# The residual moved out to DRAM during the expert stage, and a fourth expert's first weights loaded into its place

## The reference, cut to what matters

```
x2 = x + concat(RMSNorm_A(attention), RMSNorm_B(conv)) @ W_out
h  = RMSNorm(x2)
group = argmax(h @ w_group)                       # 1 of 4
two experts of the 8 in the group, by h @ w_expert, with gates
for each chosen expert e:
    hid = silu(h @ w_gate[e]) * (h @ w_up[e])     # 1024 -> 512
    y  += gate * (hid @ w_down[e])                # 512 -> 1024
out = RMSNorm_final(x2 + y)
```

## Time and profile before

| | us |
|---|---|
| median of 3 runs | 884.88 (883.33 to 888.36) |
| profiled execution | 884.24 |
| its span in the trace | 882.4 |
| TensorE busy | 834.6 (95%) |
| VectorE / ScalarE / GpSimd busy | 379.2 / 239.7 / 136.9 |
| queue of SyncE's transfers | 240.39 MB, 69.8% of 16 engines' span |
| HBM read / written | 247.01 MB / 24.20 MB |

### The profile page before, as it was taken

One profiled execution on the slowest core, in us unless ns is written; L12 is line 12 of the kernel. 1 busy time (PEld: TensorE's weight loads), 2 busy tenths in 40 slices (PEclk: granted clock), 3 DMA queues, 4 the chain that ended last, 5 costly groups with the idle time before them and its releaser, 6 DMA issues.

```text
span 882.4 us, 15903 instructions
## 1 busy us (share of the span) xinstructions
PE 834.6 (95%) x5910; PEld 560.5 (64%) x5911; DVE 379.2 (43%) x712; ACT 239.7 (27%) x490; POOL 136.9 (16%) x287
## 2 busy tenths in 40 slices
PE   6999999999999999899999889999999999999974
PEld 5988877778777888665555455555555555555531
DVE  5599999985563545721111111111111111111246
ACT  4423211557876133111111111111111111111122
POOL 3300110000000010121222122112221122211112
PEclk9999999999999999999999999999999999999988
DMA  7454644122171489499999999999999999999875
GB/s 194 103 134 118 192 160 167 48 85 61 48 239 49 189 349 384 169 407 418 418 420 419 420 420 421 419 421 419 421 419 420 418 421 419 420 410 419 368 288 183
DMA packets 81010, 262.42 MB, mean 297 GB/s; under 512 B 19017, under 2 KB 44873, under 8 KB 56394
## 3 DMA queue, kind: packets, MB, share of 16 engines
q1 hardware_dynamic: 62976, 240.39, 69.8%
q0 software_dynamic: 7888, 18.78, 5.5%
q10 hardware_dynamic: 10106, 2.71, 1.3%
HBM read 247.01 MB, written 24.20 MB: 307 GB/s over the span
## 4 chain that ended last, share of the span: by engine, by line
PE 53%; DMA 18%; DVE 16%; SPq 8%; issue 2%; ACT 1%; POOL 1%; POOLq 0%; DVEq 0%; ACTq 0%
DMA big<-in_w_up 16%; PE ps L1381 12%; PE ps L1418 8%; DVE big L1843 8%; SPq L804 8%; PE ps L1260 8%; PE ps L1124 7%; PE ps L1384 3%; PE ps L1396 2%; PE ps L1176 2%; PE ps L1143 2%; PE ps L1372 1%; PE ps L1155 1%; DVE w_split L1780 1%; PE ps L1469 1%
## 5 line engine op out<-in xcount | busy, mean ns | idle before, releaser
L2131 DVE TENSOR_TENSOR big<-ps,big 64x256 f32<-64x256 f32 x78 | 33.2, 426 | 380.5 <-ACT big L1700 380.4
L1384 PE MATMUL ps<-ring,big 128*64 128x256 f32 x704 | 156.1, 380 | 3.6 <-DMA ring<-in_w_up 3.4
L1381 PE MATMUL ps<-ring,big 128*64 128x256 f32 x704 | 156.2, 379 | 1.3 <-issue 1.2
L1124 PE MATMUL ps<-hT,w_split 128*128 128x256 f32 (+1 forms) x744 | 136.5, 340 | 0.5 <-DVE big L1812 0.5
L1381 PEld LDWEIGHTS ps<-ring,big 128*64 128x64 f32 x704 | 96.0, 137 | 56.6 <-issue 12.1
L1124 PEld LDWEIGHTS ps<-hT,w_split 128*128 128x128 f32 x744 | 113.0, 189 | 21.0 <-issue 7.6
L1384 PE MATMUL ps<-big 128*64 128x256 f32 x544 | 121.5, 380 | 5.1 <-DMA big<-in_w_up 5.1
L1381 PE MATMUL ps<-big 128*64 128x256 f32 x544 | 121.5, 380 | 0.0
L1384 PEld LDWEIGHTS ps<-ring,big 128*64 128x64 f32 x704 | 96.2, 137 | 8.0 <-DMA ring<-in_w_up 4.9
L1381 PEld LDWEIGHTS ps<-big 128*64 128x64 f32 x544 | 74.1, 137 | 39.2 <-issue 9.0
L1700 ACT ACTIVATE big<-ps 64x256 f32<-64x256 f32 x78 | 29.3, 375 | 245.3 <-PE ps L1384 245.3
(11 more groups left out here) (269 smaller groups left out, 1166.8 us busy)
## 6 DMA issues: line engine op xcount, KB each, us to landing
ring<-in_w_gate SPq DMA_DIRECT2D x44, 1024.0 KB, 27.5
ring<-in_w_up SPq DMA_DIRECT2D x44, 1024.0 KB, 28.3
ring<-in_w_down SPq DMA_DIRECT2D x44, 1024.0 KB, 28.7
big<-in_w_gate SPq DMA_DIRECT2D x20, 1024.0 KB, 27.7
big<-in_w_up SPq DMA_DIRECT2D x20, 1024.0 KB, 28.2
big<-in_w_down SPq DMA_DIRECT2D x20, 1024.0 KB, 28.1
w_raw<-in_w_in SPq DMA_DIRECT2D x20, 512.0 KB, 4.0
results<-spare POOLq DMA_DIRECT2D x12, 512.0 KB, 3.8
```

Source lines behind the costliest of these rows:

```text
L1124: mm = pe.matmul(ps[:, n % 2, 0:size], w_split[:, sub, hi_w, k, :], hT[:, k // 4, hi_h, k % 4, cols], **flags)
L1381: pe.matmul(ps[0:BLK, 6 * h, 0:FH], xT[:, k % (KD // 2), q, :], gate_w[s][:, k, fs], start=(k == 0), stop=(k == KD - 1))
L1384: mm = pe.matmul(ps[BLK:2 * BLK, 6 * h + 1, 0:FH], xT[:, k % (KD // 2), q, :], up_w[s][:, k, fs], start=(k == 0), stop=(k == KD - 1))
L2131: nc.vector.tensor_tensor(hb[:, fs], ps[BLK:2 * BLK, 6 * h + 1, 0:FH], sG[:, fs], ALU.mult).then_inc(hb_ready[h], 1)
```

## The change

- `AT_ONCE` is 4: experts 0 to 3 have places 0 to 3. The ranks of the other one-block places are shifted by one.
- Each tile of `x` is stored to a DRAM tensor `x2_rows` when it is complete (`keep_x2`).
- When two tiles have been stored and are no longer read, one piece of expert 3's weights is loaded into their place (`load_lent`; `lent` is a view of `x` as three pieces). The pieces are gate half 0, up half 0 and gate half 1.
- Place 3 is multiplied with these three pieces (`in_lent`) and with its other three in slot 0. The slot's own first three pieces so come free for place 6: they are loaded while place 0 ends, and place 6's other three behind place 3. From place 9 on `load_expert` is as before.
- Behind the last weights and ahead of the final gain, the six tiles of `x` are loaded back. The last stage waits for `tile_in[t]` to reach 96.

```diff
--- before.py
+++ after.py
@@ -74,10 +74,12 @@
 MAXPAIRS = (MAXB - 7) // 2
 
 
-PLACES = [((0, 3, 1), E - 3, 1), ((8, 27, 3), 6, -1), ((9, 25, 3), 12, -1), ((7, 26, 3), 19, -1), ((3, 7, 1), 20, 1), ((27, 32, 1), 24, 1)]
-AT_ONCE = 3
+PLACES = [((0, 4, 1), E - 4, 1), ((8, 27, 3), 6, -1), ((9, 25, 3), 12, -1), ((7, 26, 3), 19, -1), ((4, 7, 1), 20, 1), ((27, 32, 1), 23, 1)]
+AT_ONCE = 4
 NB = MAXB + 2
 SLOTS = 3
+
+LENT = 3
 CONSTS = 16 + len(PLACES)
 
 RPBW = 127
@@ -424,6 +426,8 @@
 
     h_rows = nc.dram_tensor("h_rows", (2 * T, D // 2), F32, kind="Internal").ap()
     results = nc.dram_tensor("results", (4 * T, D // 2), F32, kind="Internal").ap()
+
+    x2_rows = nc.dram_tensor("x2_rows", (T, D), F32, kind="Internal").ap()
     h_whole, results_whole = (a.rearrange("(r s) d -> r (s d)", s=2) for a in (h_rows, results))
 
     def rows_of(x_p, x_s, t):
@@ -511,6 +515,9 @@
         gate_w = [g[:, 0:KD * F].rearrange("p (k f) -> p k f", k=KD) for g in gus]
         up_w = [g[:, KD * F:].rearrange("p (k f) -> p k f", k=KD) for g in gus]
         down_w = [d.rearrange("p (k d) -> p k d", k=KF) for d in dns]
+
+
+        lent = x.rearrange("p t d -> p (t d)").rearrange("p (b k f) -> p b k f", b=LENT, k=KD // 2)
 
         taken_at = [(slot2_gu if t < 4 else slot2_dn)[:, 2 * (t % 4) * D:2 * (t % 4 + 1) * D].rearrange("p (j d) -> p j d", j=2)
                     for t in range(NT)]
@@ -672,6 +679,7 @@
         gate_in = [[sem(f"gate_in{s}{q}") for q in range(2)] for s in range(SLOTS)]
         up_in = [[sem(f"up_in{s}{q}") for q in range(2)] for s in range(SLOTS)]
         dn_in = [[sem(f"dn_in{s}{q}") for q in range(2)] for s in range(SLOTS)]
+        lent_in = [sem(f"lent_in{b}") for b in range(LENT)]
         xt_ps, xt_ready, y_done, y_evac = sem("xt_ps"), sem("xt_ready"), sem("y_done"), sem("y_evac")
 
         xb_in, y_out = ([sem(f"{what}{q}") for q in range(2)] for what in ("xb_in", "y_out"))
@@ -796,21 +804,28 @@
                 for q in range(2):
                     yield dn_in[s][q], down_w[s], w_down, slice(q * KF // 2, (q + 1) * KF // 2)
 
+            def weights_of(e, w, ks):
+                if w is w_down:
+                    return w[0, bass.ds(e, 1), ks.start * P:ks.stop * P, :].rearrange("e (p k) d -> p (e k) d", p=P)
+                return w[0, bass.ds(e, 1)].rearrange("e (p k) f -> p (e k) f", p=P)[:, ks, :]
+
             def load(e, landed, to, w, ks):
-                if w is w_down:
-                    src = w[0, bass.ds(e, 1), ks.start * P:ks.stop * P, :].rearrange("e (p k) d -> p (e k) d", p=P)
-                else:
-                    src = w[0, bass.ds(e, 1)].rearrange("e (p k) f -> p (e k) f", p=P)[:, ks, :]
-                sp.dma_start(to[:, ks, :], src).then_inc(landed, 16)
+                sp.dma_start(to[:, ks, :], weights_of(e, w, ks)).then_inc(landed, 16)
 
             def load_some(e, s, first, end):
                 for l in list(in_order(s))[first:end]:
                     load(e, *l)
 
+            def expert_at(place):
+                return sp.value_load(table[0:1, bass.ds(place + (3 * E + 2), 1)], min_val=0, max_val=E - 1)
+
+            def end_of(place):
+                return sp.value_load(table[0:1, bass.ds(place + 2 * E, 1)], min_val=1, max_val=MAXB)
+
             def load_expert(i, s):
                 place = SLOTS * i + s
-                e = sp.value_load(table[0:1, bass.ds(place + (3 * E + 2), 1)], min_val=0, max_val=E - 1)
-                end = sp.value_load(table[0:1, bass.ds(place + (2 * E - SLOTS), 1)], min_val=1, max_val=MAXB)
+                e = expert_at(place)
+                end = end_of(place - SLOTS)
                 sp.wait_ge(gu_half, end)
                 load_some(e, s, 0, 2)
                 sp.wait_ge(gu_done[1], end)
@@ -858,12 +873,53 @@
                 load(1, *l)
             load(0, *pieces[0][5])
 
+
+            def keep_x2(t):
+                sp.wait_ge(x2_done, OUT.index((OUT_CHUNKS - 1, t)) + 1)
+                sp.dma_start(x2_rows[t * P:(t + 1) * P, :], x[:, t, :]).then_inc(tile_in[t], 16)
+
+            def load_lent(b):
+                for t in (2 * b, 2 * b + 1):
+                    sp.wait_ge(tile_in[t], 48)
+                sp.wait_ge(sq2, 2 * b + 2)
+                sp.wait_ge(h2_ready, 2 * b + 2)
+                sp.wait_ge(x2t_done, 2 * b + 2)
+                _, _, w, ks = pieces[0][b]
+                sp.dma_start(lent[:, b], weights_of(SLOTS, w, ks)).then_inc(lent_in[b], 16)
+
+            for t in range(NT):
+                keep_x2(t)
+            for b in range(LENT):
+                load_lent(b)
+
             sp.wait_ge(table_ready, 2)
-            with sp.Fori(1, E // SLOTS) as i:
+
+            ahead, end = expert_at(2 * SLOTS), end_of(0)
+            sp.wait_ge(gu_half, end)
+            load_some(ahead, 0, 0, 2)
+            sp.wait_ge(gu_done[1], end)
+            load_some(SLOTS, 0, 3, 4)
+            load_some(ahead, 0, 2, 3)
+            sp.wait_ge(y_done, end)
+            load_some(SLOTS, 0, 4, 6)
+            for s in range(1, SLOTS):
+                load_expert(1, s)
+            ahead, end = expert_at(2 * SLOTS), end_of(SLOTS)
+            sp.wait_ge(gu_done[1], end)
+            load_some(ahead, 0, 3, 4)
+            sp.wait_ge(y_done, end)
+            load_some(ahead, 0, 5, 6)
+            load_some(ahead, 0, 4, 5)
+            for s in range(1, SLOTS):
+                load_expert(2, s)
+            with sp.Fori(3, E // SLOTS) as i:
                 for s in range(SLOTS):
                     load_expert(i, s)
             for place in range(E // SLOTS * SLOTS, E):
                 load_expert(place // SLOTS, place % SLOTS)
+
+            for t in range(NT):
+                sp.dma_start(x[:, t, :], x2_rows[t * P:(t + 1) * P, :]).then_inc(tile_in[t], 16)
 
             sp.wait_ge(gates_ps, 1)
             sp.dma_start(fin_g, bass.AP(final_g.tensor, 0, [[0, P], [1, D]])).then_inc(norms_in, 16)
@@ -1372,17 +1428,17 @@
                     mm = pe.transpose(ps[:, 4, k * P:(k + 1) * P], xb[:, k * P:(k + 1) * P], ident[:])
                 mm.then_inc(xt_ps, 1)
 
-            def gate_up(s, target, q, h):
+            def gate_up(gate, up, q, h):
 
                 fs = slice(h * FH, (h + 1) * FH)
-                for k in range(q * KD // 2, (q + 1) * KD // 2):
-                    if h == 0 and k % (KD // 2) == 0:
-                        pe.wait_ge(gate_in[s][q], target)
-                    pe.matmul(ps[0:BLK, 6 * h, 0:FH], xT[:, k % (KD // 2), q, :], gate_w[s][:, k, fs], start=(k == 0), stop=(k == KD - 1))
-                    if h == 0 and k % (KD // 2) == 0:
-                        pe.wait_ge(up_in[s][q], target)
-                    mm = pe.matmul(ps[BLK:2 * BLK, 6 * h + 1, 0:FH], xT[:, k % (KD // 2), q, :], up_w[s][:, k, fs],
-                                   start=(k == 0), stop=(k == KD - 1))
+                for k in range(KD // 2):
+                    flags = dict(start=(q == 0 and k == 0), stop=(q == 1 and k == KD // 2 - 1))
+                    if h == 0 and k == 0:
+                        pe.wait_ge(gate[0], gate[1])
+                    pe.matmul(ps[0:BLK, 6 * h, 0:FH], xT[:, k, q, :], gate[2][:, k, fs], **flags)
+                    if h == 0 and k == 0:
+                        pe.wait_ge(up[0], up[1])
+                    mm = pe.matmul(ps[BLK:2 * BLK, 6 * h + 1, 0:FH], xT[:, k, q, :], up[2][:, k, fs], **flags)
                 if q:
                     mm.then_inc(gu_done[h], 1)
                 elif h:
@@ -1397,12 +1453,22 @@
                                       hb[:, h * FH + k:(h + 1) * FH:2], ident[0:BLK, 0:BLK])
                 mm.then_inc(ht_ps[h], 1)
 
-            def expert_block(b, s, target):
+            def in_slot(s, target, head):
+
+                k0, k1 = slice(0, KD // 2), slice(KD // 2, KD)
+                return [((gate_in[s][0], head, gate_w[s][:, k0, :]), (up_in[s][0], head, up_w[s][:, k0, :])),
+                        ((gate_in[s][1], head, gate_w[s][:, k1, :]), (up_in[s][1], target, up_w[s][:, k1, :]))]
+
+            def in_lent(target):
+                return [((lent_in[0], 16, lent[:, 0]), (lent_in[1], 16, lent[:, 1])),
+                        ((lent_in[2], 16, lent[:, 2]), (up_in[0][1], target, up_w[0][:, KD // 2:KD, :]))]
+
+            def expert_block(b, s, target, halves):
 
                 pe.wait_ge(xt_ready, b + 1)
                 for q in range(2):
                     for h in range(2):
-                        gate_up(s, target, q, h)
+                        gate_up(*halves[q], q, h)
                 turn_hidden(b, 0)
 
                 pe.wait_ge(xb_copied, b + 2)
@@ -1425,12 +1491,12 @@
                 first = pe.value_load(table[0:1, bass.ds(place + E, 1)], min_val=0, max_val=MAXB - 1)
                 return n, first
 
-            def blocks(n, first, s, target):
+            def blocks(n, first, s, target, halves):
                 with pe.Fori(0, n) as j:
-                    expert_block(first + j, s, target)
-
```

(28 more changed lines are left out.)

## The result

The changed kernel takes 888.91 us (median of 10 runs, 886.58 to 890.21), the kernel before 884.66 beside it (10 runs, 883.33 to 888.36). The ratio is 1.0044 with a 95% interval of 1.0033 to 1.0056: slower by 0.44%, clear of noise with these runs and still inside the 0.5% that the prediction counted as the same. The forecast was 888.2, with a range of 882.0 to 893.0. The profiled execution took 889.17 us with a span of 887.3, which is 4.9 us more span than before.

What follows compares the result with a forecast made beforehand. The DMA engines' weight stream was taken to set the pace of the expert stage. From 884.24, -7.5 (stream), +5.9 (late start) and +5.6 (read-back) sum to +4.0: 888.2 us, range 882.0 to 893.0.

Steps and rivals of the forecast that it cites:

- 7.5 less in the stream: Expert weights after 369: three pieces, 3.15 MB, leave the stream, saving 7.5 us at 417 GB/s.
- 5.9 for a late start: Before the first blocks: slowed transfers on the router's chain delay block 0's end, block 1 and the next weight triggers by 5.9 us.
- 5.6 for the read-back: Behind the last weights: reloading 3.15 MB adds 7.5 us on the slowest DMA engine, 1.9 idle absorbs some; cost 5.6 us.
- The DMA engines set the pace: Expert stage: TensorE's 13.7 us of losses are waits for weights; an earlier or lighter stream saves time out of those.
- ScalarE's stores of h: Tiles 4 and 5, before the first gather: slowed beside x's stores, 0 to +3 us, taken as +0.9.
- The gather of block 0: Router's chain, issued at 360.1: slowed beside stores, 0 to +5.3 us, taken as +2.0, with 0.7 given back by VectorE.
- That of block 1: Second gather on the router's chain: beside the lent loads it takes 6.9 us in place of 3.2, +3.7.
- A: End of the kernel: the read-back fits before the results and the lead is kept, 882.6 to 878.6; chance 0.14.
- B: Start: gathers suffer under +1 us each, only the spill of 1.9 to 3 us is paid, 884.8, no change; chance 0.17.
- C: Start is worse: stores of h held up 3 us, gathers take 8.2, 12 us in place of 5.9, 894; chance 0.12.
- D: Expert stage: TensorE is the limit, start delay adds in full +5.9, read-back 0 to 5.6, 890 to 896; 0.09 with E.
- E: Start: x's region not free until 345, lent pieces issued behind block 0, bytes only change places, about 886 to 890; 0.09 with D.

Runs made afterwards that it cites:

- the copy later: Changed kernel with VectorE's copy of block 1's rows, and its part in block 0's first hidden half, moved behind the router's one-hot work: 886.29 us, ratio 1.0014.
- the stores alone: Kernel before plus only the six stores of x to DRAM, with no lent loads and no read-back: 889.4 us, ratio 1.0046.

## Why the prediction was right

The sum was +4.0: 7.5 less in the stream, 5.9 for a late start, 5.6 for the read-back. The trace has +4.9 of span, the medians +4.3. That the sum came so near is in part luck: the late start was sized 1.2 us too small and the read-back some 0.5 too large.

1. *The DMA engines set the pace, so a late TensorE start is not paid as such.* Right between the kernel before and the changed one: the start was 8.5 us late and the expert stage ended 0.4 early. The plainest pair is the runs with the copy later and with the lent loads behind the second gather. Block 1's turn is at 394.1 and 394.0, and block 37's at 828.6 and 834.0. What differs is the idle time of the DMA engines. These are the windows from 357 to 397 (columns as in the earlier trace rows) of the kernel before, the changed kernel, the copy later, and the lent loads behind the gather:

```profile
357.00:397.00 40.00, 37.82 (x414) 26.14 (x414) 20.60 (x68) 4.63 (x14) 8.40 (x14) 1.00 0.70 276
357.00:397.00 40.00, 33.03 (x356) 23.47 (x358) 18.11 (x64) 2.69 (x8) 6.14 (x10) 0.87 0.90 350
357.00:397.00 40.00, 34.95 (x376) 24.93 (x378) 19.90 (x67) 3.63 (x11) 7.39 (x12) 0.91 0.95 382
357.00:397.00 40.00, 34.81 (x372) 24.69 (x372) 19.58 (x67) 3.63 (x11) 7.39 (x12) 0.91 0.82 330
```

   In finer windows the idle time is 11.9 us before and 4.0 after; 7.9 won, less 7.5 for the stores, is 0.4. This account held within about 2 us for the other kernels (with the lent loads behind the gather 2.7 late by it, 1.0 measured; with the stores alone 5.2 and 4.3), not better.

   The rule has a bound that the prediction does not name. TensorE paid its late start out of its waits for weights. The 9.1 us that it lost between 473.0 and 517.9 before are gone in the changed kernel. It runs from 398 to 553 without a loss, and then loses about 1 us five times. With these waits used up, a later start is paid nearly in full. In the six runs of the changed kernel whose block 1 came at 394.0 to 396.4 (all but the one with the lent loads behind the gather), block 37 came 434.4 to 435.6 us after it; in the changed kernel it is 434.6.
2. *The start, 5.9 us.* The place and the mechanism were right, the pieces were not. ScalarE's stores of h took +0.9 in the sum. In the trace they took 12.2 us for 11.7, but were issued 0.5 us sooner and landed at 359.1 as before: nothing was lost there. The gather of block 0 was mis-sized, +2.0 for a measured 3.7 (used at 366.7 for 363.0): I had let stores slow it by half of what loads do. That of block 1 was +3.9 for the 3.7 of the sum. And the granted clock was missing. The down product of block 0 ran in part at the lower level (the line below; a product of this form took 0.59 us before). It began 6.8 us late, as VectorE's copy at 375.4 did, and ended 8.5 us late, which is the delay at block 1's turn. The stream's own delay, worked out as 7.5 less 0.4, was 7.1 in place of 5.9.

```profile
...
382.14 1.06 PE L1484 MATMUL ps<-ring,big 128*64 128x512 f32 x1
```

3. *The read-back, 5.6 us.* Near in size: 5.1 to 5.6 by taking it out, 4.3 to 5.1 by putting it alone into the kernel before. That the last engine decides, not the mean share, is inferred from the two traces together: 7.2 us of engine time idle, bytes of 7.5 us placed in it, and 4 to 6 us lost all the same. Which engines are late no view here names, so the sentence of the Trainium skill ("DMA: Bandwidth & Descriptors", Latency and other measured facts) on engines 7 and 15 stays untested.
4. *The rivals.* A hidden read-back (A) is out by two runs. B, gathers hardly slowed, is out by their 6.58 and 7.08 us. C had 8.2 us for a gather, 3 us for the stores of h and 12 us for the start, against 7.1 at most, 0.5 and 7.1. D, TensorE as the limit, is out as it stood, since 8.5 us of late start were not paid; but what is left of it is the bound in point 1. E, lent pieces issued behind block 0, is out: they were issued at 362.8, 365.6 and 368.1, ahead of the first loads that block 0 releases (374.5).
5. *The signs named.* The first two gathers in 5 to 8 us: 6.58 and 7.08. A hole of 3 to 5 us before 392: there were two, 1.8 us of idle at 373 to 377 and 1.4 at 385 to 389. Block 1's turn "at about 395": 398.0. TensorE's loss from 389 to 761 down "to about 6": between blocks 1 and 31 the turns lie 363.0 us apart, for 358.2 at 11.94 each, so 4.8. The final gain at 851 to 852: 852.6. The first sum at about 854: 855.2.

So the lead that the change wanted is there. The changed kernel ends the expert stage 4.7 us before the run with the stores alone (832.6 for 837.3), though its block 1 comes 3.1 us later; the full 7.5 us are worked out from the bytes. The lead is paid for twice on the same 16 engines, once by the way in, since the idle stretch held two gathers on the path that opens the stream, and once by the way out.

## What to carry to other kernels

Bytes that are moved out of a stream of transfers and have to come back through the same engines win only the idle time they fall into; count both ways, and count idle time on the engine that is last, by when a late small transfer in that queue lands. A later start of the compute engine costs nothing only as long as it has waits to give up. Before filling an idle stretch of the DMA engines, list the small transfers that run in it on the path to the next issue: here two gathers of 3 us became 7. And when a load is made to stand in for another in an experiment, give it the same row pitch.

## What the runs showed of the hardware

- The first two gathers of 128 rows of 2 KB landed in 2.9 to 3.7 us with nearly idle DMA engines, in 6.2 to 7.1 beside a stream: 6.16 beside stores of 4 KB rows alone, 6.58 beside stores and then loads of weights, 7.08 beside loads of weights.
- Loads of tiles whose rows lie 256 KB apart landed in a median of 33.9 us, those of rows that follow each other in 24.9, from the same place in the queue; the end came 9.9 us later. The tensors read differ too.
- TensorE's granted clock stood at half of full speed from 365 to 369, around the end of a wait of 3.6 us for a gather, and again, in part (0.62), from 381 to 385. Products of the down product took 1.06 us there for 0.59.
